# First block's attention in rounds of two steps: a transformer kernel on one core

## The reference

```python
def dense_attention(q, k, v, sink=None):
    s = gqa_logits(q, k)
    if sink is None:
        return gqa_combine(jax.nn.softmax(s, axis=-1), v)
    s = jnp.concatenate([s, sink_logits(sink, s)], axis=-1)
    p = jax.nn.softmax(s, axis=-1)[..., :-1]
    return gqa_combine(p, v)
...
        o = jnp.concatenate([
            global_attention(qa, ka, va, kac, vac),
            fourier_mix(fb),
            window_attention(qc, kc, vc, kcc, vcc, sink[l]),
        ], axis=-1)
        x = x + gt1 * (o @ w_out[l])
...
        if update_ctx:
            oc = jnp.concatenate([
                dense_attention(qac, kac, vac),
                fourier_mix(fbc),
                dense_attention(qcc, kcc, vcc, sink[l]),
            ], axis=-1)
```

## Time and profile before

| what | us |
|---|---|
| median of three runs | 1554.39 |
| the profiled execution, whole | 1555.53 |
| its span (first to last instruction) | 1553.6 |
| PE busy in the span | 1497.7 |
| attention of layer 0 on PE (from the first L1095 to `w_out`'s first product) | 107.6 to 204.6 |
| attention of layer 1 on PE | 696.3 to 756.5 |

### The profile page before, as it was taken

One profiled execution on the slowest core, in us unless ns is written; L12 is line 12 of the kernel. 1 busy time (PEld: TensorE's weight loads), 2 busy tenths in 40 slices (PEclk: granted clock), 3 DMA queues, 4 the chain that ended last, 5 costly groups with the idle time before them and its releaser, 6 DMA issues.

```text
span 1553.6 us, 23281 instructions
## 1 busy us (share of the span) xinstructions
PE 1497.7 (96%) x9195; PEld 1255.6 (81%) x9195; DVE 1083.3 (70%) x1631; ACT 674.6 (43%) x1055; POOL 131.7 (8%) x133
## 2 busy tenths in 40 slices
PE   6999999999999999998989999899999999999998
PEld 3765578888888888874789999788988988898896
DVE  2747745778887886858466667788765777877566
ACT  3445715221121212537443333655555646455463
POOL 1210002000000000410010000321000121200002
PEclk9999999999999999999999999999999999999999
DMA  9536313454445633325245555545524455463342
GB/s 335 194 106 211 91 58 133 150 172 154 142 162 211 240 115 106 94 97 136 82 136 185 186 180 180 183 163 163 183 89 136 138 182 163 144 209 109 123 141 91
DMA packets 169421, 235.85 MB, mean 152 GB/s; under 512 B 9021, under 2 KB 116581, under 8 KB 169193
## 3 DMA queue, kind: packets, MB, share of 16 engines
q1 hardware_dynamic: 169320, 234.45, 46.1%
HBM read 233.38 MB, written 1.05 MB: 151 GB/s over the span
## 4 chain that ended last, share of the span: by engine, by line
PE 82%; DVE 9%; ACT 4%; issue 2%; POOL 2%; DMA 1%; SPq 0%; POOLq 0%; DVEq 0%; ACTq 0%
PE psum L821 24%; PE psum L823 23%; PE psum L822 23%; PE psum L1095 3%; PE psum L1128 3%; DVE wl L1873 2%; PE psum L1115 2%; DVE smax L2196 1%; PE psum L836 1%; PE psum L1023 1%; PE psum L1167 1%; ACT wh L1426 1%; PE psum L955 1%; DMA raw<-in_w_ada 1%; ACT hTh L1648 1%
## 5 line engine op out<-in xcount | busy, mean ns | idle before, releaser
L1873 DVE TENSOR_TENSOR wl<-raw,wh 128x2048 fp32r<-128x2048 f32 (+1 forms) x170 | 384.7, 2263 | 161.1 <-ACT wh L1426 94.4
L821 PE MATMUL psum<-hTh,wh 128*128 128x256 f32 (+1 forms) x1376 | 430.0, 313 | 5.0 <-DVE hTl L1996 3.5
L823 PE MATMUL psum<-hTh,wl 128*128 128x256 f32 (+1 forms) x1376 | 423.1, 307 | 0.0
L822 PE MATMUL psum<-hTl,wh 128*128 128x256 f32 (+1 forms) x1376 | 423.1, 307 | 0.0
L821 PEld LDWEIGHTS psum<-hTh,wh 128*128 128x128 f32 x1376 | 262.3, 191 | 23.5 <-issue 6.9
L1763 ACT ACTIVATE wh<-raw 128x2048 fp32r<-128x2048 f32 x62 | 118.9, 1917 | 371.6 <-PE psum L823 371.6
L822 PEld LDWEIGHTS psum<-hTl,wh 128*128 128x128 f32 x1376 | 262.4, 191 | 13.3 <-issue 0.7
L823 PEld LDWEIGHTS psum<-hTh,wl 128*128 128x128 f32 x1376 | 262.2, 191 | 12.6
L1426 ACT ACTIVATE wh<-raw 128x2048 fp32r<-128x2048 f32 (+2 forms) x108 | 202.5, 1875 | 108.7 <-PE psum L823 97.8
L821 PE MATMUL psum<-wh,hTh 128*128 128x512 f32 (+3 forms) x576 | 222.0, 385 | 9.0 <-DVE hTl L1975 4.1
L823 PE MATMUL psum<-wh,hTl 128*128 128x512 f32 (+3 forms) x576 | 218.0, 379 | 0.0
(11 more groups left out here) (206 smaller groups left out, 1794.2 us busy)
## 6 DMA issues: line engine op xcount, KB each, us to landing
raw<-in_w_in SPq DMA_DIRECT2D x54, 1024.0 KB, 4.9
raw<-in_w_ada SPq DMA_DIRECT2D x24, 1024.0 KB, 5.3
raw<-in_w_gate SPq DMA_DIRECT2D x22, 1024.0 KB, 5.1
raw<-in_w_up SPq DMA_DIRECT2D x22, 1024.0 KB, 5.2
raw<-in_w_down SPq DMA_DIRECT2D x22, 1024.0 KB, 4.8
qkT<-in_w_ada SPq DMA_DIRECT2D x16, 1024.0 KB, 7.2
raw<-in_w_in SPq DMA_DIRECT2D x16, 768.0 KB, 4.5
vals<-in_w_ada SPq DMA_DIRECT2D x8, 1024.0 KB, 6.2
```

The costliest lines, as they stand in the source:

```text
L821: pe.matmul(o, left[0], right[0], start=first, stop=False)
L822: pe.matmul(o, left[0], right[1], start=False, stop=False)
L823: return pe.matmul(o, left[1], right[0], start=False, stop=last)
L1873: dve.tensor_tensor(wl[:, w % SPLIT, 0:m], raw[:, u % RING, 0:m], wh[:, w % SPLIT, 0:m].bitcast(F32), ALU.subtract).then_inc(lo_ready, 1)
```

## The change

The layers of the second block (`second`) keep their order. In the first block, PE's turns of the loop are now of two kinds. An even turn i does the logits of step i and then the values of steps i-4 and i-3, which are a pair. An odd turn does the logits of step i and then the transposes of steps i-3 and i-2, also a pair. ACT follows. In an odd turn both `keep_turned` now stand behind `probs(i)`, where before one stood in front of it. `lead` moves to the even turns, as `lead(i - 3)`. On DVE `keep_mixed(i - 4)` stands behind `shifts(i)`, where `keep_mixed(i - 5)` stood in front of it. The numbers of `BESIDE_AT` move by one place or stay. The amount of work is the same.

```diff
-BESIDE_AT = [[1, 3, 4, 5, 7, 9, 10, 12, 13, 15, 16, 18, 19, 21, 27, 31, 35, 39, 43, 46, 49, 52],
-             [1, 3, 5, 7, 19, 22, 25, 28]]
+BESIDE_AT = [[0, 2, 4, 6, 8, 9, 11, 12, 14, 15, 17, 18, 20, 21, 27, 31, 35, 39, 43, 46, 49, 52],
+             [0, 2, 4, 6, 19, 22, 25, 28]]
...
                 for i in range(len(steps) + lag + 1):
                     if i < len(steps):
                         logits(steps[i])
-                    if 0 <= i - lag < len(steps):
+                    if second and 0 <= i - lag < len(steps):
                         turn_probs(steps[i - lag])
                     next(beside, None)
                     if i == lag + 1:
                         pe.wait_ge(evac_act, vals_ready)
-                    if 0 <= i - lag - 1 < len(steps):
+                    if second and 0 <= i - lag - 1 < len(steps):
                         values(steps[i - lag - 1])
+                    if not second and i % 2 == 0:
+                        for j in (i - 4, i - 3):
+                            if 0 <= j < len(steps):
+                                values(steps[j])
+                    if not second and i % 2 == 1:
+                        for j in (i - 3, i - 2):
+                            if 0 <= j < len(steps):
+                                turn_probs(steps[j])
                     next(beside, None)
...
-                    if 0 <= i - lag < len(steps):
+                    if second and 0 <= i - lag < len(steps):
                         keep_turned(i - lag)
...
-                    if 0 <= i - behind < len(steps):
+                    if second and 0 <= i - behind < len(steps):
                         lead(i - behind)
+                    if not second and i % 2 == 0 and 0 <= i - 3 < len(steps):
+                        lead(i - 3)
+                    if not second and i % 2 == 1:
+                        for j in (i - 3, i - 2):
+                            if 0 <= j < len(steps):
+                                keep_turned(j)
...
-                    if not second and 0 <= i - 5 < n:
-                        keep_mixed(i - 5)
                     if i < n:
                         shifts(i)
+                    if not second and 0 <= i - 4 < n:
+                        keep_mixed(i - 4)
```

## The result

The changed kernel takes 1579.27 us, the median of four runs from 1577.46 to 1582.41. The kernel before took 1554.76 on the same chip (four runs, 1553.89 to 1556.70). The ratio is 1.0158, with a 95% interval of 1.0139 to 1.0177: the change made it slower by 24.5 us. The forecast was 1583 with a range of 1571 to 1591.

A forecast was written before the change was run, and what follows sets the result against it. PE, busy 96% of the span, was taken as the bound. Added waits less removed ones gave +22.0 us; less 6.8 plus 13.8 for the clock, +29.0, so 1555.5 + 29.0 - 1.1 = 1583 us, range 1571 to 1591.

The forecast's parts named there:

- What it removes: PE's waits in both layers' attention: 10.3 us for bank 6, 0.8 for last copies, 1.7 for pieces; 12.8 us gone.
- I let 1.7 us go: PE's three waits for pieces beside, 3.1 us together: 1.7 us go and 1.4 stay.
- The chain: Odd turns: second transposes wait for logits, maximum, exponentials, then ACT's copy; 14.9 us in layer 0, 16.3 in layer 1.
- It waits 2.6 us: Plain wide step in an odd turn: chain of 3.6 us, of which PE's first transposes cover 1.03.
- With mask and sink: Wide steps with mask and sink in odd turns: a longer chain of 4.35 us, a wait of 3.3 us.
- The 5.3 us of turn 7 in layer 1: Wait before second transposes, with weight splits ahead of the step on ACT and DVE: 3.3 + 2.0 us.
- The context steps had 3.6: Layer 0's context steps: values wait for copies, 0.6 us in each of six turns, 3.6 us added.
- Nothing hides this.: Both stages: PE has no other work in its list during the added waits; +22.0 us net of those removed.
- I take six falls, 13.8 us: Low clock in both attention stages: six falls at 2.3 us each, replacing three falls costing 6.8 us.
- the copies keep up: Rival: ACT finishes copies during the first step's transposes, so wide pairs wait only 0.3 us; -12.4 us, 1542 us; chance 0.02.
- The clock holds: Rival: the waits come, but the clock holds or falls twice at most; +15.2 to +19.8 us, 1570 to 1574; chance 0.12.
- Nine falls: Rival: each of nine waits of 2.3 us or more brings a clock fall; +35.9 us, 1590 us; chance 0.15.

The follow-up runs named there:

- experiment 6: The changed kernel unaltered, run again on another chip: 1582.7 us, median of four runs, ratio 1.0186.
- experiment 4: The kernel before with only the new BESIDE_AT numbers (pieces one place earlier): 1551.49 us, ratio 0.9977.
- experiment 1: The changed kernel with both steps' copies (both keep_turned) in front of the exponentials probs(i) in odd turns: 1545.73 us, ratio 0.9953.
- experiment 5: The changed kernel with one to five unread 128x512 products added before the second transposes of odd turns, filling PE's long waits: 1569.72 us, ratio 1.0103.
- experiment 2: The changed kernel with only the first step's copies in front of the exponentials, the second step's behind them: 1547.86 us, one run.
- experiment 8: The changed kernel with copies before exponentials, logits between the two transposes, and layer 1's weight splits two turns later: 1542.61 us, ratio 0.9925.
- experiment 3: The changed kernel with PE's odd turns as first step's transposes, logits, second step's transposes, ACT's order unchanged: 1592.96 us, one run.
- experiment 7: The kernel before with DVE's part alone, keep_mixed(i - 4) behind shifts(i): 1560.56 us, one run.

## Why the forecast came out as it did

The sign and the mechanism were right, and the range held the time. By the steps of the prediction, for both stages of the profiled runs:

| us | forecast | first profile | second profile (6) |
|---|---|---|---|
| waits or idle time of PE, change | +22.0 | +21.8 | +21.5 |
| lost to low clock, before | 6.8 | 5.7 | 5.7 |
| lost to low clock, changed | 13.8 | 10.5 | 15.6 |
| larger groups | 0 | -4.4 | -4.4 |
| sum | +29.0 | +22.2 | +27.0 |

The losses are differences of busy time: 142.9 - 137.2 (experiment 4 less its fall) for before; 143.3 - 132.8 and 148.4 - 132.8 (experiment 1) for the changed kernel. The last row is also what the lengths of the stages say, 179.4 - 157.2 and 184.2 - 157.2, but all rows are cut from the same busy times, so that they add up is no check of the parts. The granted clock is one: taken in windows of 0.5 us and weighted with PE's busy share, what it took from PE is 6.4 us before, 10.8 in the first profile and 14.8 in the second.

- **What it removes.** "I take all 10.3 us as gone, and the 0.8 us of the last copies too": shown. No row of L2240 is left, and of L1128 only three waits of the context steps, which were counted with the additions. "I let 1.7 us go" of the pieces: 0.9 us is left where I kept 1.4.
- **The chain.** "It waits 2.6 us" in a plain turn: 2.57 and 2.63 in the two plain turns without a piece. "With mask and sink ... 3.3": 3.38 and 3.31. The 5.3 us of turn 7 in layer 1, worked out from the split ahead of the maximum, are 5.31. The turns of layer 0 were forecast at 1.6, 2.6, 1.5, 2.8, 3.3 and 3.1 and measured 1.56, 2.63, 1.45, 2.94, 3.38 and 2.43. Those of layer 1 were forecast at 2.3, 2.6, 5.3, 3.3, 2.3 and 0.5 and measured 2.45, 2.57, 5.31, 3.31, 2.90 and 0.40. Two are off by over 0.5 us. One is the estimate of 1.5 for a split ahead of a context step, which had no row. The other, turn 11 of layer 1, is not the 1.0 for the two Fourier groups, which took 0.96. DVE was at a division and began the step 0.28 us behind the logits and not 0.11, and on ACT a high part of the Fourier branch (L1625) stood ahead of the copies, 0.27 us more. The context steps had 3.6 and took 2.3 + 1.4 = 3.7 us, in part by luck. The forecast had six waits of the values for a copy. There were three, 2.3 us, and the 1.4 are waits of the transposes for DVE's division, for which it had no term. With what stays the forecast makes 36.2 us, and the rows have 35.9.
- **"Nothing hides this."** Idle time grew by 21.8 us and the stages by 22.2.
- **The clock.** "I take six falls, 13.8 us": six came in the first profile and eight in the second. The term that was mis-sized is the price, 2.3 us each. It is 10.5 / 6 = 1.75 and 15.6 / 8 = 1.95. But by the same measure the falls of before cost 5.7 / 3 = 1.9, so the price is no smaller in the changed kernel. The forecast's 2.3 has two faults of its own. It counts the whole deficit of the clock, 6.8 us, while a part of the low time passes in waits, where it costs nothing. And it is a mean over three falls of which one is double: 1.7 us in 190 to 202, 3.4 in 720 to 740, 1.7 in 740 to 750. Counted as the forecast did, the deficit in the two stages is 11.9 us for six falls and 17.1 for eight, 2.0 and 2.1 each. The two clock terms together, +7.0 in the forecast, came to +4.8 and +9.9.
- **A term that was missing.** The sum has nothing for the groups that grow to two steps. Their 4.4 us come from experiments 1 and 4. That they come of the groups' ends is my reading of the rows. It wasn't tried apart from the rest of the change.

The two misses have the same sign, and the first median is 4.1 us under the forecast. On the chip of experiment 6, with two falls more, the median is 0.7 under 1583.4. So the nearness there owes something to falls that made up for the missing term.

Of the rivals, "the copies keep up", 1542 us, is what the order of experiment 1 gives (1545.7), so its price was near and only its condition was missing. "The clock holds" is experiment 5: it forecast +15.2 us, and +15.5 was measured. That agreement is partly luck too, since the filling overshoots by 1.8 us and the missing 4.4 stand against it. "Nine falls" would need 1590. The highest single run has 1586.23. The Trainium skill's section "HAM oscillation — how this bites in real kernels" in "TensorE: Matmul & The Clock Gate" has the clock fall at every burst of a kernel whose waits are of about 3 to 5 us. The prediction took it for waits of 2.3 us and more. In the first profile nine such waits gave six falls. In the second there were eight such waits (that of turn 13 in layer 0 was 1.78 us), and each had its fall. So falls come behind shorter waits than the section's too, but not behind each.

What the changed profile would show came as said: eleven waits over 1 us before the second transposes, 31 us in all, the longest of 5.3 in turn 7 of layer 1, the exponentials waiting for DVE. Only the lengths of the stages were off, +10.6 and +11.6 us for 14 and 15. Why the same waits of 2 to 3 us bring a fall in one run and none in another stays open: the trace shows when the clock fell, and no experiment here moved that alone.

## What to carry to other kernels

When one engine does two steps of a stage in a row, look at what the engine that frees its buffers has in front of that work in its own list. If that is work on something the first engine has only just made, the wait is the whole chain through three engines, and it comes back in each round. Here one step's two copies moved in front of two exponentials were worth over 30 us, while the two banks by themselves cost about 0.4 us a turn.

Where waits are of 2 us and more, make the sum in three parts: idle time, time at the low clock, and the products' own time. PE's busy time alone stayed the same to 0.2 us and hid two changes of opposite sign.

## What the runs showed of the hardware

- The same products take less time in longer groups: the 288 values of layer 0 took 21.0 us in 24 groups of 16 or 8 and 18.4 in 12 groups of 32 or 16, both at a granted clock of 1.00. One group of 32 took 1.97 us, two of 16 took 1.09 each.
- The time of one program follows the clock: 1577.46 to 1586.23 us over the eight runs of the changed kernel, with mean clocks from 0.989 to 0.984, while the waits of the two profiled runs differ by 0.3 us. With no idle time of PE over 1.6 us at a stretch (experiments 1, 2, 5 and 8) no fall came in either stage of the profiled runs. Over the two stages in the profiles of the kernel before, the changed kernel (both) and experiments 3, 4 and 7, a fall came at each of the 16 waits of 3.2 us or more, at 12 of the 21 waits of 2.0 to 3.0 us, and at none that was shorter.
- Unread products in the waits kept the clock at 1.00 and gave back 10.5 us of 179.4, though idle time and filling together were 37.9 us against 36.1 of idle time without it.
